# Hybrid decoder trunk on one core: mixer linears fed with undivided rows, the root applied to their results, weights numbered through both layers

## What is computed

```
h = x * rsqrt(mean(x*x) + eps) * g_mix            # RMSNorm of the layer's input
z = h @ w_in                                      # one projection, split among the branches
cq, ckv, kr, u, v, gq, gk, gv, ga, gg, gate = split_in(z)
A: latent attention from cq = rmsnorm(cq), ckv = rmsnorm(ckv), kr = rope(kr), with a paged cache
B: u * (W_s layernorm(v) + b)       C: gated linear attention from gq, gk, gv, ga, gg
x = x + (sum_j sigmoid(gate_j) * (branch_j @ W_p_j)) @ W_o
x = x + SwiGLU(rmsnorm(x)) @ W_down
```

## Time and profile before

| | |
|---|---|
| median of 3 runs | 2318.15 us (2311.84 to 2318.26) |
| the profiled execution | 2310.12 us |
| its span | 2308.4 us |
| mean granted TensorE clock | 0.965 of full speed |
| TensorE, weight loads, VectorE, ScalarE, GpSimd busy | 94%, 88%, 43%, 31%, 13% |
| DMA | 329.55 MB, mean 143 GB/s |

### The profile page before, as it was taken

How to read it: one execution, slowest core, us unless ns; L and a number is a source line. 1 busy time by engine, 2 the same in 40 slices (tenths; PEclk the granted TensorE clock), 3 DMA queues, 4 the chain that set the end, 5 groups by cost and what they waited for, 6 DMA issues and landing times.

```text
span 2308.4 us, 56282 instructions
## 1 busy us (share of the span) xinstructions
PE 2158.6 (94%) x24272; PEld 2037.8 (88%) x24272; DVE 989.6 (43%) x1537; ACT 722.9 (31%) x1107; POOL 303.9 (13%) x534
## 2 busy tenths in 40 slices
PE   5998899989999999999978979999899999999997
PEld 4897888778899999999978878887788999999997
DVE  3566321234465544442255662212355555444333
ACT  3344111324433322222143531231334333222221
POOL 0000344452000000000000014445410000000000
PEclk8998999999999999999989989999989999999999
DMA  4213788894133233333242239979921333333232
GB/s 175 83 50 97 260 278 264 285 321 156 54 120 105 89 93 94 92 87 94 58 166 66 64 115 294 287 256 321 320 61 54 125 106 90 93 92 92 85 94 70
DMA packets 164894, 329.55 MB, mean 143 GB/s; under 512 B 24371, under 2 KB 102502, under 8 KB 163494
## 3 DMA queue, kind: packets, MB, share of 16 engines
q10 hardware_dynamic: 47520, 149.97, 21.4%
q1 hardware_dynamic: 92550, 104.64, 13.8%
q0 software_dynamic: 24576, 71.34, 9.5%
HBM read 311.68 MB, written 14.17 MB: 141 GB/s over the span
## 4 chain that ended last, share of the span: by engine, by line
PE 80%; DVE 6%; DMA 6%; issue 3%; ACT 3%; SPq 1%; ACTq 0%; POOLq 0%; POOL 0%; DVEq 0%; PEldq 0%
PE PS L1653 23%; PE PS L1655 22%; PE PS L1654 22%; DMA vpg<-in_cache_vals 3%; DMA kpg<-in_cache_keys 3%; PE PS L1876 2%; PE PS L1905 2%; PE PS L1704 2%; PE PS L1880 1%; PE PS L1690 1%; DVE wl L634 1%; DVE yr L675 1%; PE PS L2055 1%; ACT wh L1237 1%; SPq L2234 1%
## 5 line engine op out<-in xcount | busy, mean ns | idle before, releaser
L1653 PE MATMUL PS<-hh,wh 128*128 128x260 f32 x3072 | 896.0, 292 | 45.5 <-DVE hl L641 26.2
L1655 PE MATMUL PS<-hl,wh 128*128 128x260 f32 x3072 | 876.7, 285 | 0.7 <-issue 0.7
L1654 PE MATMUL PS<-hh,wl 128*128 128x260 f32 x3072 | 875.9, 285 | 0.0
L1653 PEld LDWEIGHTS PS<-hh,wh 128*128 128x128 f32 x3072 | 588.0, 191 | 62.1 <-issue 34.0
L634 DVE TENSOR_TENSOR wl<-raw,wh 128x1024 fp32r<-128x1024 f32 (+3 forms) x330 | 356.4, 1081 | 581.0 <-ACT wh L1237 580.6
L1655 PEld LDWEIGHTS PS<-hl,wh 128*128 128x128 f32 x3072 | 588.1, 191 | 0.9 <-issue 0.9
L1654 PEld LDWEIGHTS PS<-hh,wl 128*128 128x128 f32 x3072 | 588.2, 191 | 0.2
L1237 ACT ACTIVATE wh<-raw 128x1024 fp32r<-128x1024 f32 (+3 forms) x330 | 309.4, 940 | 442.1 <-PE PS L1655 439.9
L1653 PE MATMUL PS<-fh,wh 128*128 128x260 f32 x704 | 198.9, 283 | 0.0
L1655 PE MATMUL PS<-fl,wh 128*128 128x260 f32 x704 | 198.7, 282 | 0.0
L1654 PE MATMUL PS<-fh,wl 128*128 128x260 f32 x704 | 198.6, 282 | 0.0
(11 more groups left out here) (310 smaller groups left out, 3023.0 us busy)
## 6 DMA issues: line engine op xcount, KB each, us to landing
raw<-in_wpack ACTq DMA_DIRECT2D x242, 512.0 KB, 3.6
kpg<-in_cache_keys SPq DMA_DIRECT2D x256, 144.0 KB, 4.0
kpg<-in_cache_keys POOLq DMA_DIRECT2D x256, 144.0 KB, 3.9
vpg<-in_cache_vals SPq DMA_DIRECT2D x256, 128.0 KB, 4.1
vpg<-in_cache_vals POOLq DMA_DIRECT2D x256, 128.0 KB, 4.7
raw<-in_wpack ACTq DMA_DIRECT2D x48, 256.0 KB, 2.7
raw<-in_wpack ACTq DMA_DIRECT2D x16, 384.0 KB, 3.2
x_keep<-xT SPq DMA_DIRECT2D x2, 2080.0 KB, 15.0
```

What stands on the lines that cost most here:

```text
L1653: pe.matmul(out, w[0], x[0], start=first, stop=False)
L1654: pe.matmul(out, w[1], x[0], start=False, stop=False)
L1655: return pe.matmul(out, w[0], x[1], start=False, stop=last)
```

## The change

- **Rows undivided.** The rows that the mixer linears take are x times gain (`scaled_row`), with no root. `rs`, the root of the layer's input, is kept until the last gate of the layer, and every result of a mixer linear is multiplied by it: by VectorE on the way out of PSUM for ckv, cq, gq, gk, gv, gg, ga and the 24 gates, in place of ScalarE's copy or activation from PSUM (Silu and Sigmoid now work in place on what VectorE wrote); by VectorE in SBUF for kr and for the four rows of u; by GpSimd for the four rows of v. Roots of cq, ckv and v are made in `var`. ScalarE squares ckv and cq from SBUF.
- **Boundary.** VectorE and ScalarE make and split the rows of the next layer's h inside the loop over `dn0` to `dn7`, as each row of x is finished. `ckv0` follows `dn7`, and the sum of the squares (`n1`) stands behind `ckv0`. There is no `layer_end`. Slabs, rings and their waits are numbered through both layers, and a group of the second layer waits for the readers of its banks in the first (`ahead`). The gains of the second layer are loaded behind the last use of the first's (`y f7`), the rotation tables behind `dn7`.
- **Start.** x comes in eight DMAs. The first two weight slabs are issued at once. ScalarE and VectorE make row k of h as soon as piece k is there, between the squares.
- **Order.** The sums of squares for `nkv` stand behind `krA`, for `nq` behind `cq2`, the third of `nq` between `v01` and `v23`; banks of `n1`, `nq`, `v01`, `v23` and `smpT` are set by hand. VectorE and ScalarE split v01 and v23 ahead of the rows of cq.

```diff
-    groups, slabs, narrow = ["n1"], [], set()
+    groups, slabs, narrow = [], [], set()
...
-    lin("ckv0", "ckv1")
+    lin("ckv0")
+    groups.append("n1")
+    lin("ckv1", "krA")
     groups.append("nkv")
-    lin("krA", "krB", "cq0", "cq1")
-    groups.append("nq")
-    lin("cq2")
-    groups.extend(["v01", "v23", "smpT"])
+    lin("krB", "cq0", "cq1", "cq2")
+    groups.extend(["nq", "v01", "v23", "smpT"])
...
+    fixed = {"n1": [6, 7], "nq": [4, 5], "v01": [6, 7], "v23": [0, 1], "smpT": [5], "q0": [6, 7], "q1": [0, 1], "bm": [3, 4], "bv": [3, 4], "ql": [3, 4], "Sn": [0]}
...
-        return f"sig {g[1:]}"
+        return f"gate {g[1:]}"
...
-            i, n = si[name], slab_columns(name)
+            i, n = S.layer * NS + si[name], slab_columns(name)
...
-                while split[0] <= min(i + AHEAD, len(slabs) - 1):
+                while split[0] <= min(max(S.layer, 0) * NS + i + AHEAD, DEPTH * NS - 1):
...
+            def scaled_row(x, k, gain, prefix, layer):
+
+                y = ynext()
+                dve.wait_ge(*own())
+                dve.tensor_scalar(y[:, :], x[:, k, :], gn[:, gain + k:gain + k + 1], None, ALU.mult).then_inc(*mark("value_ready", f"y {prefix}{k}"))
+                return y
...
+            prev = None
+            for k in range(8):
+                dve.wait_ge(*upto(f"x in {k}"))
+                y = scaled_row(xT, k, G_MIX, "h", -1)
+                if prev is not None:
+                    lo(f"h{k - 1}", [(hl[:, k - 1, :], prev[:, :], hh[:, k - 1, :])])
+                prev = y
+                if k == 1:
+                    weights(-1)
+            lo("h7", [(hl[:, 7, :], prev[:, :], hh[:, 7, :])])
...
+                def low_rank(n, dst):
+
+                    weights(si[n])
+                    dve.wait_ge(*upto(f"pe {n}"))
+                    dve.tensor_tensor(halves(dst), pair(n), halves(rs[:, :]), ALU.mult).then_inc(*mark("dve_evac", f"free {n}"))
+
                 weights(si["ckv0"])
-                weights(si["ckv1"])
+                rsqrt("n1", D, 1e-6, rs)
+                for k in range(2):
+                    low_rank(f"ckv{k}", ckvf[:, k, :])
...
-                for n in ("cq0", "cq1", "cq2"):
-                    weights(si[n])
-                rsqrt("nq", QR, 1e-6)
-                dve.wait_ge(*upto("free cq2"))
-                normed(3, lambda k: cqf[:, k, :], G_Q, cqh, cql, "cqn")
+                for k in range(3):
+                    low_rank(f"cq{k}", cqf[:, k, :])
                 weights(si["uv"])
+                rsqrt("nq", QR, 1e-6, var)
...
+                normed(3, lambda k: cqf[:, k, :], G_Q, cqh, cql, "cqn")
...
+                    elif name[:2] == "gq":
+                        dve.wait_ge(*upto("ha kept"))
+                        dve.wait_ge(*upto(f"pe {name}"))
+                        dve.scalar_tensor_tensor(halves(gqs[int(name[2])][:, :]), pair(name), 0.125, halves(rs[:, :]), ALU.mult, ALU.mult).then_inc(*mark("dve_evac", f"free {name}"))
+                    else:
+                        if name == "gk0":
+                            dve.wait_ge(*upto("ha kept"))
+                        p, e = int(name[2]), int(name[-1])
+                        dst = {"gk": gks[p][:, :], "gv": gvs[p][:, e, :], "gg": sgs[p][:, e, :]}[name[:2]]
+                        dve.wait_ge(*upto(f"pe {name}"))
+                        dve.tensor_tensor(halves(dst), pair(name), halves(rs[:, :]), ALU.mult).then_inc(*mark("dve_evac", f"free {name}"))
+                    if n == 3:
+                        dve.wait_ge(*upto("act uf"))
+                        for i in range(4):
+                            ins = dve.tensor_tensor(uf[:, i, :], uf[:, i, :], rs[:, :], ALU.mult)
+                        ins.then_inc(*mark("dve_step", "u scaled"))
...
+                def gate(j, m):
+                    dve.wait_ge(*upto(f"pe g{j}{m}"))
+                    dve.wait_ge(*own())
+                    if (j, m) == (1, 0):
+                        dve.wait_ge(*upto("lo hb3"))
+                    dve.tensor_tensor(halves(gsig[m % 2][:, :]), pair(f"g{j}{m}"), halves(rs[:, :]), ALU.mult).then_inc(*mark("gate_scaled", f"gate {j}{m}"))
...
+                    if l + 1 < DEPTH:
+                        if m == 0:
+                            dve.wait_ge(*upto("ld gains", l + 1))
+                        y = scaled_row(xT, m, G_MIX, "h", l)
+                        if prev is not None:
+                            lo(f"h{m - 1}", [(hl[:, m - 1, :], prev[:, :], hh[:, m - 1, :])])
+                        prev = y
+                if prev is not None:
+                    lo("h7", [(hl[:, 7, :], prev[:, :], hh[:, 7, :])])
...
+            load(1)
             for k in range(8):
+                act.wait_ge(*upto(f"x in {k}"))
                 if k >= 2:
                     act.wait_ge(*upto(f"first square used {k - 2}"))
                 act.activation(sq[k % 2][:, :], xT[:, k, :], ACT.Square).then_inc(*mark("first_squares", f"first square {k}"))
-            act.wait_ge(*upto("pe first sum"))
-            S.last = None
+                y = ynext()
+                hi(f"h{k}", [(hh[:, k, :], y[:, :])], [f"y h{k}"])
+                if k == 1:
+                    weights(-1)
+            load(RAW_RING - 1)
...
-                    act.activation(halves(gsig[m % 2][:, :]), pair(f"g{j}{m}"), ACT.Sigmoid).then_inc(*mark("act_evac", f"sig {j}{m}"))
+                    act.wait_ge(*upto(f"gate {j}{m}"))
+                    act.activation(gsig[m % 2][:, :], gsig[m % 2][:, :], ACT.Sigmoid).then_inc(*mark("act_step", f"sig {j}{m}"))
...
+                    if name[:2] == "gg":
+                        act.wait_ge(*upto(f"free {name}"))
+                        dst = sgs[int(name[2])][:, int(name[3]), :]
+                        act.activation(dst, dst, ACT.Silu).then_inc(*mark("act_step", f"silu {name}"))
...
-                act.sem_inc(S.sem("layer_end"), 1)
-                act.wait_ge(S.sem("layer_end"), 5 * l + 5)
-            S.last = None
+                        if l + 1 < DEPTH:
+                            y = ynext()
+                            hi(f"h{m - 1}", [(hh[:, m - 1, :], y[:, :])], [f"y h{m - 1}"])
...
+                if l:
+                    begin("n1")
+                    row_sum("n1", lambda b: bank("n1", b)[:, 0:HT], "nx", l - 1)
+                else:
+                    done_groups[0] += 1
...
                 linear("ckv1", ["ckv1"], hh, hl)
+                linear("krA", ["krA"], hh, hl)
                 begin("nkv")
...
+                linear("cq2", ["cq2"], hh, hl)
                 begin("nq")
                 add_square("nq", True, False)
-                linear("cq2", ["cq2"], hh, hl)
                 add_square("nq", False, False)
-                add_square("nq", False, True)
                 pe.wait_ge(*upto("lo ckvn1"))
                 for i, g in enumerate(("v01", "v23")):
+                    if i:
+                        add_square("nq", False, True)
                     begin(g)
...
+            for k in range(8):
+                sp.dma_start(xT[:, k, :], a["x_t"][:, k, :]).then_inc(*mark(f"x_loaded{k}", f"x in {k}", 16))
...
+                if l:
+                    sp.wait_ge(*upto("y f7", l - 1))
+                    sp.dma_start(gn[:, :], a["gains"][bass.ds(l, 1), :, :].rearrange("a p c -> p (a c)")).then_inc(*mark("gains_loaded", "ld gains", 16))
+                    sp.wait_ge(*upto("pe dn7", l - 1))
...
+                    pool.tensor_tensor(vf[:, k, :], vf[:, k, :], rs[:, :], ALU.mult).then_inc(*mark("pool_step"))
```

261 lines of the change are left out of this document (123 added, 138 removed).

## The result

| | kernel before | changed kernel |
|---|---|---|
| median of the runs beside the first profile | 2316.36 us (4 runs, 2311.84 to 2318.26) | 2281.72 us (4 runs, 2274.26 to 2287.16) |
| ratio, 95% interval | | 0.9851 (0.9817 to 0.9885) |
| repeated beside the experiments | 2317.57 us (11 runs) | 2289.51 us (6 runs, 2280.49 to 2293.35), ratio 0.9877 (0.9854 to 0.9900) |
| profiled execution, its span | 2310.12, 2308.4 us | 2278.99, 2277.3 us |

The change makes the kernel 1.2 to 1.5% faster, 28 to 35 us. The forecast was 2276 us, the range 2264 to 2293. The experiments marked "one run" have one execution each, and for them the time says little.

A forecast was written before the change was run, and what follows sets the result against it. TensorE, busy 94% of the span, was taken as the bound, so only its idle or slow-clock time could be won. Terms: 17.9 + 17.3 + 9.5 - 4.4 - 1.4 = 38.9 us off 2314.6, so 2276 us; range 2264 to 2293.

The forecast's parts named there:

- The start: Kernel start, up to the end of `ckv0`: x in pieces and root off the path gain 17.9 us, bounds 12.5 and 18.3.
- The boundary: Between the layers, `dn7` to the end of `ckv0`: gain 17.3 us, including the slow clock; lower bound 14.
- The end of the cq rows: From the end of `cq2` to `q0`: new order gains 9.5 us for both layers, bounds 3 and 12.
- The end of the key stage: New product before `nms` makes ScalarE 2.15 us late, passed on in full: minus 4.4 us for both layers, bounds 0 and 7.
- The gates: 24 new VectorE products per layer: twenty cost nothing, slab of `g20` comes late, minus 0.7 us twice, bounds 0 and 3 each.
- Thirteen products of branch C: New VectorE products in branch C fall where VectorE mostly waits for keys; no cost was put in the sum.
- GpSimd's products: Four products and three sums over v have linears u0 to u2, 17 us, before `bm` wants them; no cost in the sum.
- The signs of being wrong: Wrong if TensorE's waits for VectorE's products out of PSUM exceed 10 us, or a layer start keeps a gap over 5 us.
- The second: Rival for the start: x pieces land one after another, the eighth at 30.6; start gives 6.5 us, time 2287; chance 0.06.
- the third: Rival: VectorE's in-order list becomes the bound, 82 products, 57 us; 12 us slower, 2327; chance 0.05.
- the fourth: Rival: the meeting was no wait, start and boundary give little, time stays within 0.3%; chance 0.04.
- The first: Rival: half only; start and boundary give 13 and 14, key stage costs 7; gain some 20, to 2295; chance 0.20.

The follow-up runs named there:

- meet: Changed kernel with the meeting of the five engines between the layers put back: 2289.37 us, 0.9868 of the kernel before; boundary 4.5 us longer.
- late: Changed kernel with the second layer's rows of h made behind the dn loop, not within it: 2291.96 us, 0.9895 of the kernel before; boundary 5.6 us longer.
- abs: Changed kernel with ScalarE reading the bank of `at` behind the second of its eight exponentials, not the eighth: 2271.70 us, one run.
- dbl: Changed kernel with each of the 48 products of a gate with the root made twice: 2295.25 us, 0.9917 of the kernel before.
- spat: Changed kernel with VectorE's spatial mixing ahead of the product of `gq1` in the key stage: 2279.72 us, one run.
- v_dve: Changed kernel with the four v rows' products by the root on VectorE out of PSUM, not GpSimd, and four ScalarE copies dropped: 2280.74 us, one run.
- x_one: Changed kernel with x loaded in one DMA in place of eight: 2290.84 us, 0.9878 of the kernel before; start 4.3 us longer than in the repeated trace.

## Why the prediction was right, and where not

- **The start**, 17.9 us: measured 18.2. The first row came at 7.39 and not 5.5, because a piece takes 6 us to land among the others and not 3.7; the pace was 1.2 us a row and not 1.4, and the table load lay ahead of x. The errors cancel, which is luck: last square summed at 21.4, forecast 20.4.
- **The boundary**, 17.3: measured 17.3, no idle time, no slow clock. The runs meet and late show that it needs both the missing meeting and the rows made beside `dn`.
- **The end of the cq rows**, 9.5 for both layers: measured 8.8. The new waits came at 0.8 us (`nq`) and 0.6 in two parts (`q0`), per layer, forecast about 1 each. What the text did not name as late next is the slab of `v1`: a step of 1.4 to 2.4 us at that place, 0.6 before.
- **The end of the key stage**, minus 4.4: measured 4.5 in the mean, though single traces have 0 to 4.5 in the second layer. ScalarE's list is late as forecast: from its last slab to `sn` it took 2.4 us before (400.73 to 403.16) and takes 4.5 now.

```profile
400.73 0.62 ACT L1237 ACTIVATE wh<-raw 128x512 fp32r<-128x512 f32 x1
```

```profile
380.58 0.62 ACT L1301 ACTIVATE wh<-raw 128x512 fp32r<-128x512 f32 x1
...
385.11 0.30 ACT L1478 ACTIVATE sn<-sn,nms 128x8 f32<-128x8 f32 x1
```

  How TensorE pays for it is not as forecast. The wait before the transposes was to be 4.9 us in each layer; it is 2.3 and 3.9 in one trace and 3.9 and 1.1 in the other (before 2.7 and 1.2, 1.2 and 2.7), and why it takes one length or another in the same kernel stays open. Another 0.9 us per layer stand earlier, at a product that comes late, and were not named:

```profile
383.18 0.39 PE L1704 MATMUL PS<-hh,wh 128*128 128x260 f32 x1 [0.87 <-DVE sg L933]
```

  And TensorE needs nothing of ScalarE's list there but one bank; abs shows it. So the 4.5 is near the 4.4 in part by luck.
- **The gates**, minus 1.4: measured 3.3, mis-sized. The slab of `g20` is waited for, 0.8 to 0.9 us per layer, forecast 0.7. "Twenty come where VectorE has half its time free: no cost" fails where ScalarE's sigmoid, now late by a product, has TensorE's work behind it. `AT`, a tile of branch C that ScalarE copies behind that sigmoid, is such a place, here in the changed kernel and then before; with the product doubled (dbl) the wait of 1.64 grows by another 0.7:

```profile
588.39 0.66 PE L1755 MATMUL PS<-ident,zz 128*128 128x128 f32 x4 [1.64 <-ACT AT L1536]
```

```profile
604.99 0.66 PE L1704 MATMUL PS<-ident,zz 128*128 128x128 f32 x4 [0.73 <-ACT AT L1487]
```

- **Thirteen products of branch C "fall where VectorE mostly waits for keys"**: this step failed. The product of `gq1` is free, the wait in front of it is not, since the spatial mixing stood behind it. Minus 6.9 us, shown by spat. Its own rule, to name what is queued behind a new wait, was applied to `nms` and not here.
- **GpSimd's products "have 17 us"**: this step failed too. They were never waited for, but by all signs they hold VectorE up: minus 3.9 us in the scores, of which v_dve gives back 3.6 (with ScalarE's four copies gone as well).
- The sum: 38.9 less 6.9, 3.9 and 1.9 (the gates) is 26.2; with the small errors of the other terms it is the 26 of the ledger. Two terms put at nothing were worth 10.8 us together. That the time still fell into the range is owed to the width of the range, which leaves 17 us above 2276. The forecast took the 38.9 from 2314.6, the mean of four executions, and the medians of the kernel before came out at 2316.36 and 2317.57; so 2276 is 6 to 14 us too low. The lower end of the range was reckoned from bounds given as 2269, but the terms' upper bounds (18.3, 17.3, 12, no losses) give 47.6 us, so 2267; nothing hangs on it.
- **The signs of being wrong** did not come. TensorE's waits for products by the root out of PSUM add up to 8.6 us (`gsig` 5.3, `sg` 1.7, `cqf` 1.6), under the 10 named, and 5.3 of them stand where 6.1 stood for ScalarE's sigmoid before. At the layer starts the only gap of over 5 us is the 8.2 us until TensorE has a first square to sum, which the forecast's own sum contains (5.5 + 1.3 + 0.64). VectorE reads `ckv0` at 27.2, forecast about 26.
- **Rivals.** The second falls by the start itself (last square summed at 21.4, where the rival had the last piece landing at 30.6) and by x_one, the third by the sign of the result and by dbl, the fourth by the 17.3 us of the boundary and by meet. The first, a gain of 20 us, lies 8 to 15 us under what was measured, the forecast 4 to 11 above it, and the reasons of the first did not come: start and boundary gave what was forecast, and the key stage cost 4.5 and not 7.

## What to carry to other kernels

When work moves from one engine to another, look at each new wait on the receiving engine and at what already stood behind it; the duration of the moved instruction says little. A wait on a bank is named by the instruction that freed it, so read back what that instruction stood behind: here one read moved ahead of six exponentials is worth more than the change had cost there. Where runs scatter by more than an effect, compare start times of the same matmul across traces.

## What the hardware showed that was not expected

GpSimd holds VectorE up. A low part of a slab (two operands in the state buffer) took 1.37 us in place of 0.55 when it began 0.36 us behind a GpSimd product of 1.31, and 2.06 in place of 1.22 when it began 0.34 us behind a sum. Both end 0.13 us before the time at which they would have ended had they begun at the end of GpSimd's instruction (115.29 and 113.36). One that begins first keeps its length: 0.55 us at 80.87, with GpSimd's product from 81.30 on. The Trainium skill, page "SBUF — State Buffer", section "SBUF: two separate sides", states that the two engines share a port pair under an exclusive lock, which a VectorE instruction with two inputs in the state buffer needs against a GpSimd instruction that reads there, and that the one that starts first has it for its whole length. The trace agrees.

Behind a stop of 2.8 us TensorE's granted clock fell: in meet the boundary grew by 4.5 us, more than the stop, with 0.83 granted in that window. It does not fall behind every such stop. In the changed kernel TensorE stands idle for 2.86 us before the same matmul of both layers (the wait for `kxl`, at 176.97 and 1295.36 us); windows of 10 us that hold the stop and what follows, first layer and then second:

```profile
176.00:186.00 10.00, 9.03 (x89) 7.95 (x89) 7.80 (x18) 4.61 (x12) 2.00 (x4) 0.99 0.56 177
1294.00:1304.00 10.00, 8.64 (x70) 7.45 (x70) 6.54 (x12) 3.25 (x11) 1.95 (x4) 0.83 0.57 179
```

The granted clock is 0.99 in the one and 0.83 in the other, at the same stop in the same execution. So what a short stop costs behind itself differs from case to case, and it may be a part of why stretches with such stops differ between traces of one kernel; that was not followed up.
